# A hybrid attention block on one core: split probabilities in the last two blocks, row maxima moved by DMA, fused band operations, and a new order

## The chip, the core and the metric

The kernel runs on one core of a Trainium2 chip. The core has five engines with instruction streams of their own: TensorE (PE in the rows, PEld for its weight loads), VectorE (DVE), ScalarE (ACT), GpSimd (POOL) and SyncE (SP), which here only issues DMAs. They meet at semaphores. The metric is the device time of one execution in microseconds; lower is better.

## What is computed

One layer of a streaming encoder, 2048 positions of width 1024, in float32. Cut to what matters here:

```python
proj = jnp.einsum('bld,dc->blc', x, w_in)
qa, ka, va, ga, qi, ki, wi, qb, kb, vb, gb = jnp.split(proj, offsets, axis=-1)
# group A: an indexer scores keys, the top 256 are kept, attention over them with ALiBi
dots = jnp.einsum('bqhd,bsd->bqhs', qi_blk, ki)
score = jnp.einsum('bqh,bqhs->bqs', w_blk * idx_scale, jax.nn.relu(dots))
_, idx = lax.top_k(score, k_top)
logits = jnp.einsum('bqhd,bqkd->bqhk', q_blk, k_sel) * attn_scale - slopes * dist
p = jax.nn.softmax(logits, axis=-1)
ya = jnp.einsum('bqhk,bqkd->bqhd', p, v_sel)
# group B: a window of 2 chunks with a sink for each head
yb = sink_window_attention(qb, kb, vb, sinks, slopes[1::2])
y = jnp.concatenate([ya * jax.nn.silu(ga), yb * jax.nn.silu(gb)], axis=-1)
x = layer_norm(ALPHA * x + jnp.einsum('blc,cd->bld', y, w_out), ln_g, ln_b)
```

## The kernel before

The 2048 queries are 16 blocks (b) of 128. The work is written as pieces with names, and a planner in the kernel's file puts them in one order: each piece has an engine, an assumed duration, the pieces it needs and a preference from a table. Each engine then issues its pieces in that order, in program order, and waits on semaphores where it must. The names below are the planner's.

The first stage computes the projections (`product`, `norm`). Each product is made of three products of rounded parts (type fp32r, a value rounded to fewer bits): high x high, low x high and high x low; the parts are made on ACT (round), POOL and DVE (split). Beside it the indexer runs for pairs of blocks (p from 1 to 7): `dots` on PE, `relu` on ACT, `sum` on DVE, and then the search of the level of the 256th largest score: 32 steps a pair, `search` on DVE for one block of the pair and `sign` on ACT for the other (L1485, L1030). `masks` p ends a pair (L1503 to L1519); the masks go to DRAM and come back for their block.

Then, for each block b:

- the scan: `scan` on PE forms the logits of each head over up to 512 keys, `scan_max` on DVE adds the mask and takes the maximum in one fused instruction (L1582). `negate` (L1593 to L1596) joins the chunks' maxima and negates them, `minus_max` transposes them on PE (L1295), and `row_max` (L1603) multiplies the 8 rows by a 0/1 pattern `sel`, so that 8 rows of the operand `qa_ext` hold them, one for each head. The logits product then subtracts the maximum by itself.
- the units: for each key tile kt and half g of the heads, `logits` on PE (L1331 to L1333, at the diagonal also L1335 and L1336), `exp_a` on ACT (L1140) and `values` on PE (L1344), one product of plain float32, which the records show as two. Logits have two PSUM banks, probabilities three buffers: 272 units in all, 30 in block 14 and 32 in block 15.
- the tail: `leave_a`, `turn_a`, `y_a`, `columns_a`, `gate_a`, `store_a`.
- the band (group B): `window` on PE, `bias_b` on DVE twice a block, each an addition of the bias to 128x768 (L1562) and a maximum over it (L1564), `max_b` (L1569), `exp_b`, `turn_b`, `copy_b`, `mix_b`, `y_b`, `columns_b`, `gate_b`, `store_b`.

Behind the last values product stands the output product (L1390) with the layer norm.

## Time and profile before

| | |
|---|---|
| time, median of 3 runs | 1541.97 us (1541.08 to 1542.38) |
| the profiled execution | 1540.4 us, span 1538.6 us |
| PE busy | 1419.8 us (92%) |
| DVE busy | 1192.4 us (78%) |
| ACT busy | 932.3 us (61%) |
| POOL busy | 419.0 us (27%) |
| mean granted clock of PE | 0.967 of full speed |

The profile is of one execution. A busy share is an average over the whole span; what an engine waits for, and in which stage, is in the views of the trace. The granted clock is the share of full speed at which PE may run; below 1 the same product takes longer.

### The profile page before, as it was taken

The page shows a single profiled execution, that of the slowest core. Times are in us where ns is not written, and L with a number is a line of the kernel's source. Part 1 is how long each engine was busy: PE and PEld are TensorE (multiplying, and loading weights), DVE is VectorE, ACT ScalarE, POOL GpSimd, SP SyncE. Part 2 cuts the span into 40 slices and gives each one's busy share as a digit, 9 for nine tenths or more (in the row PEclk, how much of TensorE's full clock was granted, in tenths as well). Part 3 has the DMA queues.
Part 4 walks back from the last instruction along what each step waited for, and adds up shares of the span by engine and source line. Part 5 has one row for each costly group of instructions (what it writes and reads, how often), then busy time and mean ns, then how long its engine had stood idle before and what let it go on. Part 6 is the DMA issues. An engine that isn't in the chain of part 4 may idle for free.

```text
span 1538.6 us, 19197 instructions
## 1 busy us (share of the span) xinstructions
PE 1419.8 (92%) x6469; PEld 1031.3 (67%) x6520; DVE 1192.4 (78%) x2235; ACT 932.3 (61%) x1797; POOL 419.0 (27%) x268
## 2 busy tenths in 40 slices
PE   6998999799999976788999989999999999989997
PEld 5887888588787765455656656556565664468886
DVE  3477878879988967989999998999998770047776
ACT  3484966865964978457969746887995634301010
POOL 3332313643234324314122121121212601012221
PEclk9999999999999996798999999999999999999999
DMA  7331231531325245312132230222314412034442
GB/s 241 97 109 62 82 93 55 164 124 44 107 84 137 86 113 120 102 34 55 47 82 55 61 94 11 60 59 61 75 32 128 129 38 66 0 116 145 142 151 81
DMA packets 104306, 136.34 MB, mean 89 GB/s; under 512 B 6499, under 2 KB 81127, under 8 KB 103951
## 3 DMA queue, kind: packets, MB, share of 16 engines
q1 hardware_dynamic: 91344, 93.16, 22.0%
q10 hardware_dynamic: 9216, 31.20, 5.3%
q0 software_dynamic: 3648, 10.76, 2.3%
q8 instruction: 52, 0.85, 0.2%
q14 instruction: 46, 0.37, 0.1%
HBM read 92.76 MB, written 42.34 MB: 88 GB/s over the span
## 4 chain that ended last, share of the span: by engine, by line
PE 61%; DVE 17%; issue 8%; ACT 6%; POOL 4%; DMA 3%; ACTq 0%; SPq 0%; POOLq 0%; DVEq 0%
PE psum L1201 18%; PE psum L1390 9%; PE psum L1344 9%; PE psum L1272 4%; DVE above L1485 3%; PE psum L1332 3%; ACT above L1030 3%; PE psum L1333 3%; DVE score L1513 2%; PE psum L1217 2%; PE psum L1331 2%; PE psum L1232 2%; POOL w_lo L853 2%; PE psum L1234 2%; DMA x_raw<-xT 1%
## 5 line engine op out<-in xcount | busy, mean ns | idle before, releaser
L1485 DVE TENSOR_SCALAR_CACHE_REDUCE above<-dist,trial 128x512 bf16<-128x512 int32 (+13 forms) x224 | 345.9, 1544 | 6.1
L1030 ACT ACTIVATE above<-dist,trial 128x384 bf16<-128x384 int32 (+13 forms) x224 | 280.9, 1254 | 43.7 <-DVE trial L1458 27.1
L1201 PE MATMUL psum<-x_hi,w_hi 128*128 128x512 f32 x640 | 253.8, 397 | 32.4 <-DVE x_lo L1527 11.7
L1344 PE MATMUL psum<-prob,vw 128*65 128x512 f32 x544 | 270.2, 598 | 0.0
L1140 ACT ACTIVATE prob<-psum 128x512 f32<-128x512 f32 x272 | 158.4, 592 | 160.3 <-PE psum L1344 143.8
L1201 PE MATMUL psum<-x_lo,w_hi 128*128 128x512 f32 x640 | 251.2, 393 | 0.0
L1201 PE MATMUL psum<-x_hi,w_lo 128*128 128x512 f32 x640 | 251.1, 392 | 0.0
L1582 DVE CUSTOM_DVE_ANT_0 junk<-psum,mask 128x512 bf16<-128x512 f32 (+3 forms) x320 | 184.0, 606 | 21.7 <-PE psum L1275 11.4
L1201 PEld LDWEIGHTS psum<-x_hi,w_hi 128*128 128x128 f32 x640 | 121.3, 190 | 64.6 <-POOL w_lo L853 16.3
L1332 PE MATMUL psum<-qa_mix,ka_mix 128*128 128x512 f32 x272 | 162.0, 595 | 1.0 <-DVE qa_ext L1603 1.0
L1272 PE MATMUL psum<-ka_ext,qa_ext 128*128 128x512 f32 (+3 forms) x320 | 137.2, 470 | 19.1 <-DVE part_max L1582 10.4
L1201 PEld LDWEIGHTS psum<-x_hi,w_lo 128*128 128x128 f32 x640 | 121.3, 189 | 26.1
L1201 PEld LDWEIGHTS psum<-x_lo,w_hi 128*128 128x128 f32 x640 | 121.5, 190 | 24.0
L1064 ACT ACTIVATE relu<-psum 128x1024 f32<-128x1024 f32 (+1 forms) x76 | 71.1, 956 | 97.8 <-PE psum L1234 59.4
L845 POOL CAST w_hi<-raw 128x1024 fp32r<-128x1024 f32 x40 | 52.5, 1312 | 262.2 <-PE psum L1201 252.2
L1344 PEld LDWEIGHTS psum<-prob,vw 128*65 128x65 f32 x544 | 72.0, 138 | 62.9 <-issue 39.8
L1333 PE MATMUL psum<-qa_ext,ka_ext 128*128 128x512 f32 x272 | 109.3, 402 | 0.0
L853 POOL TENSOR_TENSOR w_lo<-raw,w_hi 128x1024 fp32r<-128x1024 f32 x40 | 106.0, 2649 | 5.8
L980 ACT ACTIVATE yt_hi<-yt_raw 128x1024 fp32r<-128x1024 f32 x16 | 16.9, 1059 | 148.4 <-PE psum L1390 117.5
L1390 PE MATMUL psum<-wo_hi,yt_hi 128*128 128x512 f32 x256 | 101.1, 395 | 5.2 <-POOL yt_lo L951 5.1
L1434 DVE SCALAR_TENSOR_TENSOR score<-relu,vw,score 128x512 f32<-128x512 f32 (+1 forms) x114 | 91.5, 803 | 12.0 <-ACT relu L1064 5.2
L1390 PE MATMUL psum<-wo_lo,yt_hi 128*128 128x512 f32 x256 | 100.7, 393 | 0.0
(154 smaller groups left out, 2818.0 us busy)
## 6 DMA issues: line engine op xcount, KB each, us to landing
raw<-w_tiles SPq DMA_DIRECT2D x40, 512.0 KB, 4.3
proj<-staged ACTq DMA_DIRECT2D x40, 512.0 KB, 3.6
qb_raw<-proj SPq DMA_DIRECT2D x32, 256.0 KB, 3.9
qa_raw<-proj SPq DMA_DIRECT2D x32, 256.0 KB, 4.4
yt_raw<-y_t SPq DMA_DIRECT2D x16, 512.0 KB, 5.2
x_row<-x_res SPq DMA_DIRECT2D x16, 512.0 KB, 3.9
out<-z ACTq DMA_DIRECT2D x16, 512.0 KB, 2.6
x_raw<-xT SPq DMA_DIRECT2D x12, 512.0 KB, 5.0
```

Source lines behind the costliest of these rows:

```text
L853: nc.gpsimd.tensor_tensor(w_lo[:, u, :, :].rearrange("p k c -> p (k c)"), raw[:, u, :], w_hi[:, u, :, :].bitcast(F32).rearrange("p k c -> ...
L1030: nc.scalar.activation(above[:, 0, 0:n], src, ACT.Sign, scale=-1.0, bias=u, accum_out=count[:, 0:1]).then_inc(sign_counted, 1)
L1140: nc.scalar.activation(prob[:, unit % 3, :], psum[:, 4 + unit % 2, :], ACT.Exp, scale=0.125).then_inc(a_prob, 1)
L1201: last = pe.matmul(psum[:, 2 * u + m, :], wt[:, u, k, :], xt[:, k, 512 * m:512 * m + 512], start=(k == 0 and q == 0), stop=(k == KT - 1 an ...
L1272: last = pe.matmul(psum[:, bank, 0:w], qa_ext[:, s, h, :], ka_ext[:, s, c:c + w], start=True, stop=not diag)
L1332: pe.matmul(o, ka_mix[:, ks], flat(qa_mix[:, s, hs, :]), start=False, stop=False)
L1333: last = pe.matmul(o, ka_ext[:, s, ks], flat(qa_ext[:, s, hs, :]), start=False, stop=(kt < b))
L1344: pe.matmul(psum[0:65, 6 + g, :], vw[:, kt, 0:65], prob[:, u % 3, :], start=(kt == 0), stop=(kt == b)).then_inc(a_used, 1)
L1390: last = pe.matmul(psum[:, 4 + 2 * s + m, :], yt[:, s, k, :], wt[:, k, cols], start=(k == 0 and q == 0), stop=(k == KT - 1 and q == 2))
L1434: v.scalar_tensor_tensor(o, relu[:, h, 0:w], wt, o, ALU.mult, ALU.add).then_inc(summed, 1)
L1485: v.tensor_scalar(above[:, 1, 0:n], src, u, None, ALU.is_ge, ALU.add, accum_out=count[:, 1:2]).then_inc(own_counted, 1)
L1582: v.tensor_tensor_reduce(out=junk[:, scan % 2, 0:w], in0=psum[:, scan % 2, 0:w], in1=mask[:, s, c:c + w], scale=1.0, scalar=-3.0e38, op0=A ...
```

## The change

Five things are changed together.

1. In blocks 14 and 15 (`SPLIT_FROM = 14`) the values product is made of three products of rounded parts. ACT computes the exponential twice, once in float32 and once rounded (`prob_hi`); the difference `prob_lo` is made on POOL for g = 0 and on DVE for g = 1 (`low_a`). The parts of the values are made once on POOL (`split_values`).
2. Row maxima: the multiplication by `sel` is gone. The maxima are transposed as they are (`turn_max`), DVE negates 8x128 of them into `minus_max` (`leave_max`), and SP moves these by DMA into one row of `qa_ext` (`place_max`). The negations ahead of the transposition are gone; up to block 3 the scan's maxima go straight to the transposed tile, from block 4 on one reduction (`top_of_chunks`) stays. The load and the copies of `sel` are gone.
3. `bias_b` adds and takes the maximum in one fused instruction for each head (four a half), and `y_a` has one reciprocal and one multiplication in place of two each.
4. `setup_dve` no longer waits for the last stores of the projections; the first `scan_max` does.
5. The DMA scratch is 2048 bytes a partition in place of the default. The assumed durations and the table of preferences are new, and a second table (`MOVE`) moves pieces against a first order. All pieces are put in a new order by this.

```diff
+SPLIT_FROM = 14
...
+                split = b >= split_from
+                add("ACT", 1.2 if split else 0.6, "exp_a", *unit, needs=[("logits", *unit), ("values", *unit_list[-3][1:])])
+                if split:
+                    add(*(("POOL", 1.33) if g == 0 else ("DVE", 0.66)), "low_a", *unit,
+                        needs=[("exp_a", *unit), ("low_a", *unit_list[-2][1:])])
+                add("PE", 0.66 if split else 0.86, "values", *unit,
+                    needs=[("exp_a", *unit), ("low_a", *unit), ("split_values", 1), ("leave_a", b - 1),
+                           ("values", *unit_list[-1][1:])])
...
+def first_ranks(plan):
+
+    base = whole_plan(NB)
+    first = base.timed(base.urgency())
+    like = {"low_a": lambda *unit: ("exp_a", *unit), "split_values": lambda i: ("split_qa", 8)}
+    return {piece: -first[like[piece[0]](*piece[1:]) if piece[0] in like else piece] for piece in plan.pieces}
+
...
+            def place_max(b):
+
+                sp.wait_ge(a_left_max, b + 1)
+                sp.dma_start(qa_ext[HD:HD + 1, b % 2, :, :].rearrange("p h q -> p (h q)").bitcast(F32),
+                             minus_max[:, :].bitcast(F32)) \
+                    .then_inc(a_ext, 16)
+
...
+            def split_values(i):
+                if i == 0:
+                    pool.wait_ge(norm_out, NB)
+                    settled()
+                    nc.gpsimd.tensor_copy(values_hi[:, :, :], vw[:, :, 0:65]).then_inc(values_hi_ok, 1)
+                    latest[0] = (values_hi_ok, 1)
+                else:
+                    settled()
+                    nc.gpsimd.tensor_tensor(values_lo[:, :, :], vw[:, :, 0:HD], values_hi[:, :, 0:HD].bitcast(F32),
+                                            ALU.subtract).then_inc(values_lo_ok, 1)
+                    latest[0] = (values_lo_ok, 1)
+
+            def low_a(b, kt, g):
+                u = units_to(b - 1) + 2 * kt + g
+                pool.wait_ge(a_prob, u + 1)
+                settled()
+                nc.gpsimd.tensor_tensor(prob_lo[:, u % 3, :], prob[:, u % 3, :],
+                                        prob_hi[:, u % 3, :].bitcast(F32), ALU.subtract).then_inc(a_low[0], 1)
+                latest[0] = (a_low[0], split_unit(b, kt) + 1)
+
...
-                nc.scalar.activation(prob[:, unit % 3, :], psum[:, 4 + unit % 2, :], ACT.Exp,
-                                     scale=0.125).then_inc(a_prob, 1)
+                last = nc.scalar.activation(prob[:, unit % 3, :], psum[:, 4 + unit % 2, :], ACT.Exp,
+                                            scale=0.125)
+                if b >= SPLIT_FROM:
+                    last = nc.scalar.activation(prob_hi[:, unit % 3, :], psum[:, 4 + unit % 2, :], ACT.Exp, scale=0.125)
+                last.then_inc(a_prob, 1)
...
-            def minus_max(b):
-
-                pe.wait_ge(a_neg, b + 1)
-                pe.transpose(psum[:, 0, 0:P], neg_max[:, :], ident[:, :]).then_inc(a_negt, 1)
+            def turn_max(b):
+
+                pe.wait_ge(a_scanned, scans_to(b))
+                if b >= 4:
+                    pe.wait_ge(a_top, b - 3)
+                if b == 0:
+                    pe.wait_ge(setup_pool, 2)
+                pe.transpose(psum[:, 0, 0:P], row_top[:, :], ident[:, :]).then_inc(a_turned_max, 1)
 
...
-                pe.matmul(psum[0:65, 6 + g, :], vw[:, kt, 0:65], prob[:, u % 3, :],
-                          start=(kt == 0), stop=(kt == b)).then_inc(a_used, 1)
+                if b < SPLIT_FROM:
+                    pe.matmul(psum[0:65, 6 + g, :], vw[:, kt, 0:65], prob[:, u % 3, :],
+                              start=(kt == 0), stop=(kt == b)).then_inc(a_used, 1)
+                    return
+                if (b, kt, g) == (SPLIT_FROM, 0, 0):
+                    pe.wait_ge(values_hi_ok, 1)
+                    pe.wait_ge(values_lo_ok, 1)
+                pe.matmul(psum[0:65, 6 + g, :], values_hi[:, kt, :], prob_hi[:, u % 3, :], start=(kt == 0), stop=False)
+                pe.matmul(psum[0:HD, 6 + g, :], values_lo[:, kt, :], prob_hi[:, u % 3, :], start=False, stop=False)
+                pe.wait_ge(a_low[g], split_unit(b, kt) + 1)
+                pe.matmul(psum[0:65, 6 + g, :], values_hi[:, kt, :], prob_lo[:, u % 3, :],
+                          start=False, stop=(kt == b)).then_inc(a_used, 1)
 
...
             def bias_b(b, g):
                 j0 = HD if b == 0 else 0
-                hs = slice(4 * g, 4 * g + 4)
                 dve.wait_ge(b_logits, 2 * b + g + 1)
                 if b:
                     dve.wait_ge(b_turned, 2 * b)
-                ps = psum[:, 2:4, 0:2 * WIN].rearrange("p b (h j) -> p b h j", h=2)[:, :, :, j0:WIN]
-                two = lambda t, j: t[:, hs, :].rearrange("p (b h) j -> p b h j", h=2)[:, :, :, j + j0:j + WIN]
                 if (b, g) == (0, 0):
                     dve.wait_ge(bias_in, 16)
                 if g == 0:
                     dve.wait_ge(sink_put, b + 1)
-                v.tensor_tensor(two(lb, HD), ps, two(bias, 0), ALU.add).then_inc(b_biased, 1)
-                dve.wait_ge(b_biased, 2 * b + g + 1)
-                small(v.tensor_reduce(mb[:, hs], lb[:, hs, HD + j0:HD + WIN + 1], AX_X, ALU.max))
+                for i in range(4):
+                    h = 4 * g + i
+                    last = v.tensor_tensor_reduce(out=lb[:, h, HD + j0:HD + WIN],
+                                                  in0=psum[:, 2 + i // 2, WIN * (i % 2) + j0:WIN * (i % 2) + WIN],
+                                                  in1=bias[:, h, j0:WIN], scale=1.0, scalar=sink8[:, h:h + 1],
+                                                  op0=ALU.add, op1=ALU.max, accum_out=mb[:, h:h + 1])
+                last.then_inc(b_biased, 1)
 
             def max_b(b):
                 if b:
                     dve.wait_ge(b_exp, 2 * b)
+                dve.wait_ge(b_biased, 2 * b + 2)
                 v.tensor_scalar(nmb[:, :], mb[:, :], -0.125, None, ALU.mult).then_inc(b_max, 1)
...
+                if scan == 0:
+                    for i in range(2):
+                        dve.wait_ge(stored[i], 16 * N_TILES)
...
+                top = part_max[:, h, c // 512:c // 512 + 1] if b >= 4 else row_top[:, h:h + 1]
                 v.tensor_tensor_reduce(out=junk[:, scan % 2, 0:w], in0=psum[:, scan % 2, 0:w],
                                        in1=mask[:, s, c:c + w],
                                        scale=1.0, scalar=-3.0e38, op0=ALU.add, op1=ALU.max,
-                                       accum_out=part_max[:, h, c // 512:c // 512 + 1]).then_inc(a_scanned, 1)
-
-            def negate(b):
+                                       accum_out=top).then_inc(a_scanned, 1)
+
+            def top_of_chunks(b):
                 dve.wait_ge(a_scanned, scans_to(b))
-                if b == 0:
-                    dve.wait_ge(setup_pool, 2)
-                n_chunks = 1 + b // 4
-                if n_chunks > 1:
-                    small(v.tensor_reduce(neg_max[:, 0:H], part_max[:, :, 0:n_chunks], AX_X, ALU.max))
-                    v.tensor_scalar(neg_max[:, 0:H], neg_max[:, 0:H], -1.0, None, ALU.mult).then_inc(a_neg, 1)
-                else:
-                    v.tensor_scalar(neg_max[:, 0:H], part_max[:, :, 0], -1.0, None, ALU.mult).then_inc(a_neg, 1)
-
-            def row_max(b):
-                s = b % 2
-                dve.wait_ge(a_negt, b + 1)
-                if b == 0:
-                    dve.wait_ge(setup_act, 1)
-                v.tensor_tensor(qa_ext[HD:HD + H, s, :, :], psum[0:H, 0, 0:P].unsqueeze(1).broadcast_to([H, H, P]),
-                                sel[:, :, :], ALU.mult).then_inc(a_ext, 1)
+                v.tensor_reduce(row_top[:, 0:H], part_max[:, :, 0:1 + b // 4], AX_X, ALU.max).then_inc(a_top, 1)
+
+            def leave_max(b):
+                dve.wait_ge(a_turned_max, b + 1)
+                if b:
+                    dve.wait_ge(a_ext, 16 * b)
+                v.tensor_scalar(minus_max[:, :], psum[0:H, 0, 0:P], -1.0, None, ALU.mult).then_inc(a_left_max, 1)
 
             def den_b_of(b):
                 dve.wait_ge(b_exp, 2 * b + 2)
...
+            def low_a(b, kt, g):
+                u = units_to(b - 1) + 2 * kt + g
+                dve.wait_ge(a_prob, u + 1)
+                v.tensor_tensor(prob_lo[:, u % 3, :], prob[:, u % 3, :], prob_hi[:, u % 3, :].bitcast(F32),
+                                ALU.subtract).then_inc(a_low[1], 1)
...
-    nc = bacc.Bacc("TRN2", target_bir_lowering=False, num_devices=1)
+    nc = bacc.Bacc("TRN2", target_bir_lowering=False, num_devices=1, dynamic_dma_scratch_size=2048)
```

PE's order in the middle of block 15. Before, the mask's product (L1331), the two logits products and then one values product, of the unit four ahead of these logits:

```order
L1344 MATMUL psum<-prob,vw 65x512
L1331 MATMUL psum<-ident,mask 128x512
L1332 MATMUL psum<-qa_mix,ka_mix 128x512
L1333 MATMUL psum<-qa_ext,ka_ext 128x512
L1344 MATMUL psum<-prob,vw 65x512
```

and now:

```order
L1424 MATMUL psum<-prob_hi,values_hi 65x512
L1425 MATMUL psum<-prob_hi,values_lo 64x512
L1427 MATMUL psum<-prob_lo,values_hi 65x512
L1404 MATMUL psum<-ident,mask 128x512
L1405 MATMUL psum<-qa_mix,ka_mix 128x512
L1406 MATMUL psum<-qa_ext,ka_ext 128x512
L1424 MATMUL psum<-prob_hi,values_hi 65x512
L1425 MATMUL psum<-prob_hi,values_lo 64x512
L1427 MATMUL psum<-prob_lo,values_hi 65x512
```

Three products stand where one stood; the turn of logits and values is the same.

DVE's order at the end of the scan of block 12, inside the search of the last pair (the row with `above,count` and the two behind it are one search step; "ISA" rows are the fused instruction and the read of its result). Before:

```order
L1582 ISA junk,part_max<-psum,mask 128x128
L1582 ISA part_max 128x1
L1593 TENSOR_REDUCE neg_max<-part_max 128x8
L1594 TENSOR_SCALAR neg_max<-neg_max 128x8
L1562 TENSOR_TENSOR lb<-psum,bias 128x4x192
L1564 TENSOR_REDUCE mb<-lb 128x4
L1569 TENSOR_SCALAR nmb<-mb 128x8
L1603 TENSOR_TENSOR qa_ext<-psum,sel 8x1024
```

and now:

```order
L1669 ISA part_max 128x1
L1676 TENSOR_REDUCE row_top<-part_max 128x8
L1568 TENSOR_SCALAR above,count<-dist,trial 128x2048
L1572 TENSOR_SCALAR accept<-count 128x1
L1575 TENSOR_SCALAR trial<-accept,trial 128x1
L1682 TENSOR_SCALAR minus_max<-psum 8x128
L1568 TENSOR_SCALAR above,count<-dist,trial 128x2048
L1572 TENSOR_SCALAR accept<-count 128x1
L1575 TENSOR_SCALAR trial<-accept,trial 128x1
```

The large multiplication became a small negation, and what stands between the reduction and it is a search step in place of half a band block.

SP's queue about the maxima of blocks 8 and 9, now. The new entry is `qa_ext<-minus_max`; whatever stands behind it is issued after it:

```order
L816 DMA qa_ext<-minus_max 1x8x128
L810 DMA mask<-masks 128x1280
L773 DMA qb_raw<-proj 64x8x128
L775 DMA kb_raw<-proj 64x2x192
```

Here the mask of block 9 and the queries of a band block stand behind the maxima of block 8.

## Rows read from the trace of the kernel before

**Rows 1.** The page: busy time by engine, and the chain that ended last.

```profile
PE 1419.8 (92%) x6469; PEld 1031.3 (67%) x6520; DVE 1192.4 (78%) x2235; ACT 932.3 (61%) x1797; POOL 419.0 (27%) x268
...
PE 61%; DVE 17%; issue 8%; ACT 6%; POOL 4%; DMA 3%; ACTq 0%; SPq 0%; POOLq 0%; DVEq 0%
```

**Rows 2.** Busy time by stretch; columns as in the first line.

```profile
core 0: us, PE busy (x) PEld busy (x) DVE busy (x) ACT busy (x) POOL busy (x), PEclk, DMA share, GB/s
...
580.00:1178.00 598.00, 544.97 (x2511) 350.72 (x2551) 553.71 (x1110) 446.52 (x847) 132.72 (x96) 0.95 0.25 62
1178.00:1262.00 84.00, 82.06 (x424) 55.59 (x429) 62.54 (x159) 45.52 (x98) 32.58 (x19) 1.00 0.36 109
1262.00:1354.00 92.00, 91.89 (x316) 48.10 (x320) 5.08 (x13) 33.55 (x54) 6.26 (x4) 1.00 0.10 32
```

**Rows 3.** Waits of DVE, 571 to 1178 us: in total, times, longest.

```profile
DVE junk L1582 <- PE psum L1275: 8.5, 14, 1.5
DVE mask L1542 <- DMA proj<-staged: 7.8, 1, 7.8
```

**Rows 4.** Busy time by stretch, the beginning of the middle stage.

```profile
580.00:600.00 20.00, 10.41 (x42) 9.35 (x43) 17.92 (x48) 17.82 (x43) 11.41 (x7) 0.50 0.62 131
600.00:720.00 120.00, 100.61 (x438) 65.66 (x443) 104.28 (x202) 74.41 (x124) 30.45 (x20) 0.90 0.24 61
```

**Rows 5.** Groups of DVE instructions by shape: busy us, mean ns, idle before.

```profile
L1564 DVE TENSOR_REDUCE mb<-lb 128x4 f32<-128x772 f32 x30 | 28.7, 957 | 1.0
L1562 DVE TENSOR_TENSOR lb<-psum,bias 128x768 f32<-128x768 f32 x30 | 28.6, 954 | 10.0 <-PE psum L1248 9.7
...
L1603 DVE TENSOR_TENSOR qa_ext<-psum,sel 8x1024 fp32r<-8x1024 f32 x16 | 19.5, 1216 | 1.6 <-PE psum L1295 1.1
...
L1582 DVE CUSTOM_DVE_ANT_0 junk<-psum,mask 128x256 bf16<-128x256 f32 x32 | 13.2, 419 | 5.1 <-PE psum L1275 5.1
...
L1594 DVE TENSOR_SCALAR neg_max<-neg_max 128x8 f32<-128x8 f32 x12 | 3.2, 266 | 0.4
...
L1596 DVE TENSOR_SCALAR neg_max<-part_max 128x8 f32<-128x8 f32 x4 | 2.1, 522 | 0.1
```

**Rows 6.** The timeline of DVE at 584.8 us: start, duration.

```profile
584.77 0.28 DVE L1582 CUSTOM_DVE_ANT_0 junk<-psum,mask 128x128 bf16<-128x128 f32 x1
...
584.98 0.28 DVE L1582 CUSTOM_DVE_ANT_0 junk<-psum,mask 128x128 bf16<-128x128 f32 x1
```

**Rows 7.** DMA issues: size, median us from issue to landing.

```profile
sink<-sinks SPq DMA_DIRECT2D x1, 4.0 KB, 3.1
...
ka_ext<-c_pos POOLq DMA_DIRECT2D x1, 2.0 KB, 3.6
```

**Rows 8.** The timeline of PE and ACT inside block 15.

```profile
1303.69 1.02 PE L1344 MATMUL psum<-prob,vw 128*65 128x512 f32 x2
...
1304.81 0.60 ACT L1140 ACTIVATE prob<-psum 128x512 f32<-128x512 f32 x1 [0.94 <-PE psum L1344]
...
1305.22 1.02 PE L1344 MATMUL psum<-prob,vw 128*65 128x512 f32 x2
1305.65 0.10 PEld L1331 LDWEIGHTS psum<-ident,mask 128*128 128x128 bf16 x1 [0.29 <-ACT prob L1140]
1306.08 0.38 PE L1331 MATMUL psum<-ident,mask 128*128 128x512 bf16 x1
...
1306.34 0.60 ACT L1140 ACTIVATE prob<-psum 128x512 f32<-128x512 f32 x1 [0.93 <-PE psum L1344]
```

**Rows 9.** The chain in order of time, one stretch of rounded products.

```profile
384.31 19.12 PE psum L1201 x84
```

**Rows 10.** The timeline of ACT at 1293 us: two exponentials in a row.

```profile
1293.36 1.06 ACT L1140 ACTIVATE prob<-psum 128x512 f32<-128x512 f32 x2
```

**Rows 11.** Groups of subtractions by shape, on POOL and on DVE.

```profile
L862 POOL TENSOR_TENSOR x_lo<-x_raw,x_hi 128x1024 fp32r<-128x1024 f32 x8 | 19.1, 2384 | 11.0 <-ACT x_hi L980 10.6
...
L1527 DVE TENSOR_TENSOR x_lo<-staged,x_hi 128x1024 fp32r<-128x1024 f32 x4 | 4.9, 1221 | 2.1 <-ACT x_hi L980 2.1
```

**Rows 12.** One line of DVE: duration ns shortest/median/longest.

```profile
L1569 DVE TENSOR_SCALAR nmb<-mb x16: 157/302/1894, 592.1 to 1245.8; 128x8 f32<-128x8 f32 x16
```

157 lines of the change are left out of this document (84 added, 73 removed).

## The prediction

> **What bounds the kernel now.** I read the page's busy shares and its chain first. PE is busy 92% of the span, DVE 78%, and the chain that ended last is PE for 61% and DVE for 17% [rows 1]. That is an average over stages, so the next view is the busy time of each engine by stage [rows 2]. The reader is to see five stages. Up to 560 us stand the input products, which the change touches only in their order. From 580 to 1178 stand searches, scans, bands and the units of blocks 0 to 12: PE is busy 545.0 of 598 us, DVE 553.7 of 598. From 1178, when the last mask is there, to 1262 PE is busy 82.1 of 84, and to 1354, where only the units of block 15 and the last of block 14 are left, 91.9 of 92. The rest is the output product, unchanged.
>
> In the middle stage, which of two nearly full engines sets the pace? The waits of DVE from 571 to 1178 us say it: the largest are 8.5 us on scans and 7.8 us once on the last stores (just ahead of 580) [rows 3]. Of the 44 us in which DVE has nothing running in the stage, most are the small steps between its own dependent instructions. PE is idle for 53 us there, and it also runs below full clock: 0.50 granted from 580 to 600 us, 0.90 from 600 to 720 [rows 4]. At a lower clock PE needs more time for the same work, so its true need is smaller than 545 us. So DVE sets the time at which the last mask is made, and PE the 176 us behind it.
>
> **The change part by part.** The sum is made against the profiled execution, 1540.4 us with a span of 1538.6; the median of the runs shown, 1542.0, lies 1.6 us higher, and I add that at the end.
>
> *Band operations on DVE.* Before, each half of a band block costs an addition of 0.954 us and a maximum of 0.957 us [rows 5]. Ahead of the last mask stand 26 halves: 26 x 1.91 = 49.7 us. Now each half is four fused ones of 128x192. The same kind of instruction takes 0.419 us at 128x256 [rows 5] and 0.28 us at 128x128, where the next starts 0.21 us behind it [rows 6]. Halfway in width that is 0.35 us, and 0.07 less from start to start: 0.28 at best, and 0.36 at worst, if a little of waiting comes to it. I take 0.32. The new order puts 28 halves ahead of the last mask: 28 x 4 x 0.32 = 35.8 us. Difference -13.9 (-18 to -9).
>
> *Row maxima.* The multiplication of 8x1024 that spreads the maxima costs 1.216 us a block [rows 5]; 14 stand ahead of the last mask, 17.0 us. In its place DVE negates 8x128 out of PSUM, which no row shows; the nearest small ones are 0.266 and 0.522 us [rows 5], and nothing at all would be below any row. I take 0.27: 3.8 us, difference -13.2 (-17.0 to -9.7). The old negations go: 10 x 0.266 + 4 x 0.522 = -4.7. The two DVE pairs of the tail that become one, and the reduction that stays, I count at nothing.
>
> So DVE has 31.8 us less ahead of the last mask (24 to 40). What does the stage get of it? PE's idle time there would fall from 53 to 21 us if all came through, and then PE's own waits count more often. I take four fifths, -25.
>
> *The last stores.* DVE no longer waits for them before its constants, 7.8 us [rows 3], but the first maximum of a scan still does, and the scans behind it wait for the same loads. In the new order five search steps stand between. Between 0 and -7.8 I take -2.
>
> *The path of the maxima.* From the transposition to the first unit of the block there stood one DVE instruction of 1.216 us. Now there are the negation (0.27), the issue on SP, and a transfer from 8 partitions to one. Of the small transfers one of 2 KB takes 3.6 us from issue to landing and the 4 KB of the sinks 3.1 [rows 7]; this one has 4 KB, so I take 3.1 and 3.6 as the upper end; under 1.2 it would be no loss, which no row comes near. The path is 0.27 + 3.1 - 1.2 = 2.2 us longer a block. The Trainium skill (DMA: Bandwidth & Descriptors, the table of where a transfer's time goes) gives a fixed cost of about 2.0 us to any transfer; by it the path would be some 1.1 us longer. PE has work between the transposition and the first unit in all blocks but 0, 1, 2, 4, 6, 10 and 12, where it is short (two or three scans, turns or index products). There PE waits up to 2.2 us more, 15 us at most, while DVE goes on with searches. That is in the fifth I took off. Behind the new SP entry its own queue stands still as well: loads of queries, gates and masks are issued later. They are mostly asked for a block ahead, so I take nothing.
>
> *The units of blocks 14 and 15.* A unit now starts 1.53 us after the one before (1303.69 to 1305.22), of which the values product has 0.86 (1305.22 to 1306.08) [rows 8]. Rounded products cost 19.12 / 84 = 0.228 us each [rows 9], three of them 0.68. Bound by PE, a unit would take 1.35, 0.18 less; 62 units make 11 us. But ACT now computes the exponential twice, and a pair in a row takes 1.06 us [rows 10]. PE's order is values u, logits u+4; these logits need the exponential of u+2, and that one the buffer which values u-1 frees. The loop over two units is: 0.26 from the end of that values product to ACT's start (1306.08 to 1306.34), 1.06 for ACT, 0.24 from ACT's end to the next weight load (1305.41 to 1305.65), 0.10 for that load, and a unit of 1.35: 3.01, or 1.51 a unit. The 0.24 may hold a wait of PE's own, so 1.51 is an upper value and 1.35 the lower; I take 1.49, near the loop and 0.04 less than before, for the 47 units that stand alone: -2. The 15 of block 14 that the new order puts beside scans get the full 0.18: -3. The low parts (POOL about 1.2 us, half of the 2.384 of 128x1024; DVE half of 1.221 [rows 11]) have more than a unit of time before their product, so they cost only behind the last one: +1. Together -4; the ends are -11 (PE bound) and +3 (an ACT pair of 1.2 us).
>
> A small DVE instruction of 8 columns takes between 0.157 and 1.894 us in this trace [rows 12]: something holds it. The Trainium skill (SBUF — State Buffer, on the shared port pair) says that VectorE with two SBUF inputs and a GpSimd instruction that reads SBUF exclude each other for a whole instruction, which the new subtractions on both engines would. Were each of the 31 on DVE held for a product of 1.2 us, that is 37 us of DVE time in stages where it is busy 62.5 of 84 and 5.1 of 92 us [rows 2], so nearly all of it would stay hidden. The smaller DMA scratch and the first 560 us I count at nothing, with +-3 for the new order.
>
> Sum: -25 - 2 - 4 = -31, so 1509.4 by the profiled execution and 1511 by the median.
>
> **The rivals.** *PE becomes the bound in the middle stage.* For it speaks that PE is at 91% there and gets new waits; against it its low clock, which leaves it time. If half of DVE's saving is lost (16 us) and the units give 2: about 1524, and up to 1539.
>
> *All passes, and PE's clock comes back.* The stage loses DVE's 37 us or more, and the stretches with a clock of 0.50 and 0.90 shrink (they cost half of 10.4 and a tenth of 100.6 us [rows 4], 15 us of PE time). With 8 us at the stores and 6 at the units: about 1490.
>
> *Slower: the maxima's transfer.* If no work covers it, 14 blocks x 2.2 = 31 us, as much as DVE saves; with PE's order standing still behind it and SP's loads late, each block of the middle stage costs 3 us or more. It decides once the exposed wait is over 2.2 us a block in every block. That gives about 1550. Against it speaks the work that stands between in half of the blocks.
>
> *Nothing.* The saving is eaten by these waits exactly: 1542.
>
> **How the numbers follow.** My forecast (1497 to 1524) gets 0.58, PE as the bound (1524 to 1539) 0.14, the better case (under 1497) 0.11, nothing 0.06, slower 0.11. The likeliest is 1511. The range from 1494 to 1541 leaves out most of the better case (0.08) and the slower one (0.11). Faster by over 0.2%, which is about what a measurement of this kernel can tell: 0.58 + 0.14 + 0.11 = 0.83; within it 0.06; slower 0.11.
>
> **What would show it.** The last mask at 1150 us instead of 1178 (right if at 1145 to 1160); fused band instructions of 0.30 to 0.36 us; units of block 15 at 1.46 to 1.52 us; 170 us from the last mask to 1354's counterpart instead of 176. Wrong would be: waits of PE for the new transfer of more than 15 us in sum; units above 1.55 us; a last mask later than 1170 us.

## The result and the profile after

The changed kernel takes 1529.28 us (median of 4 runs, 1527.82 to 1531.2) against 1542.18 (4 runs beside it): a ratio of 0.992, 95% interval 0.9906 to 0.9934. That is 12.9 us less, where 31 were forecast. The profiled execution of the changed kernel has a span of 1526.0 us, 12.6 less than before.

The page of the changed kernel, busy time by engine and the chain that ended last, answers to [rows 1]:

```profile
span 1526.0 us, 19664 instructions
...
PE 1411.9 (93%) x6530; PEld 1039.8 (68%) x6582; DVE 1183.7 (78%) x2410; ACT 959.2 (63%) x1857; POOL 458.1 (30%) x301
...
PE 60%; DVE 15%; ACT 12%; issue 6%; DMA 3%; POOL 2%; SPq 1%; ACTq 0%; DVEq 0%; POOLq 0%
```

DVE's busy time fell by only 8.7 us, but 24.0 us of new low parts are in it, so the edits took 32.7 us away over the whole kernel. The prediction counted 31.8 ahead of the last mask alone. There, from the start to the end of the last mask, DVE is busy 974.0 us instead of 997.9, 23.9 less; with the same code in before's order it is 968.2. So the new order puts more of DVE's other work ahead of the mask. PE's busy time fell by 7.9 us. The groups of DVE by shape (count, busy us, mean ns, idle before) answer to [rows 5]:

```profile
L1642 DVE CUSTOM_DVE_ANT_0 lb<-psum,bias,sink 128x192 f32<-128x192 f32 x120 | 42.9, 414 | 6.2 <-PE psum L1317 5.8
L1710 DVE TENSOR_TENSOR prob_lo<-prob,prob_hi 128x512 fp32r<-128x512 f32 x31 | 24.0, 774 | 45.6 <-ACT prob_hi L1209 45.5
```

The fused band instructions start every 0.34 us (604.90, 605.24, 605.58 in the timeline), near the 0.32 that was forecast.

Busy time by stretch, with the stages cut at the changed kernel's own marks, answers to [rows 2]:

```profile
core 0: us, PE busy (x) PEld busy (x) DVE busy (x) ACT busy (x) POOL busy (x), PEclk, DMA share, GB/s
580.00:1173.00 593.00, 545.20 (x2508) 350.45 (x2547) 526.61 (x1230) 458.25 (x878) 142.40 (x97) 0.96 0.24 62
1173.00:1262.00 89.00, 85.79 (x441) 58.80 (x449) 60.06 (x183) 51.55 (x99) 45.55 (x28) 0.98 0.41 128
1262.00:1345.00 83.00, 81.72 (x369) 51.03 (x374) 22.22 (x38) 51.67 (x94) 31.15 (x25) 1.00 0.04 13
```

The first line is the failure in one row. In the middle stage DVE is busy 526.6 us instead of 553.7, PE 545.2 instead of 545.0, and the stage is 593 us long instead of 598. DVE's 27 us became 22 us of idle time and 5 us of gain. The last mask is ready at 1173.1 us, the end of the second entry below, where the prediction had 1150. The same instruction ended at 1179.7 us before, so it came 6.6 us earlier, where 28 were forecast:

```profile
1163.55 5.03 DVE L1599 SCALAR_TENSOR_TENSOR dist<-score,dist 128x4096 f32<-128x4096 int16 x1
1168.62 4.47 DVE L1602 TENSOR_SCALAR above<-dist,trial 128x2048 bf16<-128x2048 f32 x2
```

What DVE waits for now, from 571 to 1173 us (total, times, longest), beside [rows 3]:

```profile
DVE junk L1669 <- PE psum L1341: 12.2, 17, 2.3
DVE junk L1669 <- PE psum L1344: 9.4, 10, 2.5
DVE junk L1669 <- issue: 5.9, 1, 5.9
DVE lb L1642 <- PE psum L1317: 4.7, 4, 1.8
```

The wait for the last stores (7.8 us) is gone, and nothing took its place: the first maximum of the scans starts at 578.5 us right behind a search step. The single wait of 5.9 us is another one, at 629.4 us, ahead of the first maximum of block 3, whose product starts at 628.7. All waits of DVE for PE in this stage together are 36.2 us; before they were 23.3. The scans' products, PE's, are the largest part of them.

To see where the gain is, I took three marks from the timelines: the start of the first product of a unit with the keys (F), the end of the last mask (M), and the start of the last such product (Z). Of the 12.6 us between the two profiles, 5.4 lie ahead of F (599.7 and 594.3 us), 1.2 between F and M (580.0 and 578.8), 3.8 between M and Z (158.3 and 154.5) and 2.2 behind Z. The profiles of kernels that are alike up to F put it anywhere from 592 to 601 us, so the 5.4 is rough; on average it is 595.7 in six profiles with the changed kernel's first part and 599.6 in four with before's, 3.9 us. The stage from which 25 us were to come gave 1.2.

### The profile page after: what moved, and what is told of

Its sections match the earlier page's. It is cut to its first block, busy times and chain, and to the rows that moved or that the text cites. A ratio compares the mean times of both kernels' runs of the same rounds, so it can differ in the third digit from the quotient of the medians.

```text
span 1526.0 us, 19664 instructions
## 1 busy us (share of the span) xinstructions
PE 1411.9 (93%) x6530; PEld 1039.8 (68%) x6582; DVE 1183.7 (78%) x2410; ACT 959.2 (63%) x1857; POOL 458.1 (30%) x301
## 4 chain that ended last, share of the span: by engine, by line
PE 60%; DVE 15%; ACT 12%; issue 6%; DMA 3%; POOL 2%; SPq 1%; ACTq 0%; DVEq 0%; POOLq 0%
PE psum L1270 17%; PE psum L1473 9%; PE psum L1418 7%; ACT above L1097 5%; PE psum L1341 4%; DVE above L1568 4%; PE psum L1405 3%; PE psum L1406 3%; PE psum L1404 2%; PE psum L1301 2%; PE psum L1286 2%; PE psum L1303 2%; DVE score L1596 2%; ACT accept L1103 2%; DVE score L1517 2%
## 5 line engine op out<-in xcount | busy, mean ns | idle before, releaser
L1418 PE MATMUL psum<-prob,vw 128*65 128x512 f32 x420 | 207.2, 595 | 1.8 <-ACT out_a L1047 1.8
L891 POOL CAST w_hi<-raw 128x1024 fp32r<-128x1024 f32 x40 | 43.5, 1087 | 297.1 <-PE psum L1270 290.8
L1341 PEld LDWEIGHTS psum<-ka_ext,qa_ext 128*128 128x128 f32 x320 | 62.4, 201 | 74.4 <-DVE part_max L1669 41.8
L899 POOL TENSOR_TENSOR w_lo<-raw,w_hi 128x1024 fp32r<-128x1024 f32 x40 | 102.3, 2557 | 5.8
```

What stands on the lines that cost most here:

```text
L899: nc.gpsimd.tensor_tensor(w_lo[:, u, :, :].rearrange("p k c -> p (k c)"), raw[:, u, :], w_hi[:, u, :, :].bitcast(F32).rearrange("p k c -> ...
L1341: last = pe.matmul(psum[:, bank, 0:w], qa_ext[:, s, h, :], ka_ext[:, s, c:c + w], start=True, stop=not diag)
L1418: pe.matmul(psum[0:65, 6 + g, :], vw[:, kt, 0:65], prob[:, u % 3, :], start=(kt == 0), stop=(kt == b)).then_inc(a_used, 1)
```

## The experiments

Theories at the start: the prediction's (DVE's work sets the time of the middle stage), the order of the changed kernel (it ate the gain, or made it), and TensorE's own work. The ratios are against the kernel before, 1542 us; differences of two ratios are given in us of it, with +-3 to 5 us by the intervals. F to M is from the profiled execution. "Low", the time at the lower clock, is explained further down; it is the mean of the timed runs.

| kernel | ratio, 95% interval | F to M, us | low, us |
|---|---|---|---|
| before | 1 | 580.0 | 102 |
| changed | 0.992, 0.9906 to 0.9934 | 578.8 | 98 |
| after_oldorder | 0.9997, 0.9979 to 1.0015 | 578.1 | 110 |
| before_in_new_order | 1.0146, 1.0124 to 1.0168 | 596.4 | 112 |
| in_new_order_fused | 1.0136, 1.0119 to 1.0153 | 597.4 | 121 |
| after_nosplit | 0.997, 0.9956 to 0.9983 | 579.4 | 101 |
| after_oldband | 0.9975, 0.996 to 0.999 | 586.5 | 110 |
| before_split | 1.0018, 1.0006 to 1.003 | 582.9 | 107 |
| before_fused | 0.996, 0.9944 to 0.9976 | 576.1 | 102 |
| before_maxima | 1.003, 1.0006 to 1.0054 | 584.9 | 108 |
| before_more_dve | 1.0067, 1.0044 to 1.009 | 592.9 | 107 |
| before_less_dve | 0.9984, 0.997 to 0.9998 | 577.3 | 102 |
| before_less_both | 0.996, 0.9939 to 0.9982 | 579.1 | 107 |
| after_more_dve | 0.9995, 0.9983 to 1.0007 | 588.4 | 100 |
| after_more_pe | 0.9952, 0.9936 to 0.9968 | 587.6 | 98 |
| after_less_dve | 0.9927, 0.9899 to 0.9954 | 579.9 | 105 |
| after_less_pe | 0.9945, 0.9927 to 0.9963 | 581.8 | 120 |
| after_less_both | 0.9909, 0.9889 to 0.9928 | 576.8 | 114 |
| after_filled_waits | 0.9899, 0.9882 to 0.9915 | 574.5 | 88 |
| after_filled_waits2 | 0.9888, 0.9871 to 0.9905 | 575.1 | 82 |

**Code and order taken apart.** The pieces' order was written out as a list and given to the other code.

```diff
-    order = planned_order()
+    order = written_order()
```

> The whole change, but its pieces in the order of before, each low part of a probability placed directly behind its exponential. Theory 1 (the order ate the gain): 1508 to 1520, the saving of VectorE comes back. Theory 2 (TensorE's work fills the time): as the changed kernel, 1524 to 1534. The prediction's theory: about 1511 to 1515, since 25 us of VectorE's saving should pass in either order.

Measured 0.9997, nothing gained: neither the prediction's 1511 to 1515 nor the first theory's 1508 to 1520, and worse than the changed kernel by 12 us. The second theory's 1524 to 1534 missed too.

> The code of before (band in two instructions a half, row maxima by a product on VectorE, one product with the values) in the order of the changed kernel; the two set-up pieces stand a few searches later, since before's set-up waits for stores that the changed kernel's does not. The changed code in before's order gained nothing (0.9997 of before) and the changed kernel without the split is at 0.997. Theory 1 (the order is itself the gain: it fills TensorE's short waits, whatever the code): 1533 to 1538, all of the gain that is not the split. Theory 2 (the order gains only with the time that VectorE has been freed): 1543 or more, slower than before, since VectorE would have 32 us more work ahead of the last mask, in an order made for less.

Measured 1.0146, +22.5 us: theory 2. So the same order costs before's code 22 us and gives the changed code 12. One caution: with the list word for word, before's code would wait for itself for ever. It needs its two set-up pieces later and a semaphore more, and its first unit starts at 607 us; 16 of the 22 us lie between F and M.

**One part at a time, in before's order.** The band's edit as in the diff; the split of the last two blocks as in the diff, each low part directly behind its exponential; the maxima's edit as in the diff, and with it the shorter set-up, the joined pairs of `y_a` and the small scratch.

> The kernel before with one edit of the change alone, the fused band instructions, in before's order: 14 us less of VectorE spread over all 16 blocks. The prediction's theory: -11, 1531. A1 (one-sided): 0 to -4. Undoing this edit in the changed kernel cost 8.5 us.

Measured 0.996, -6.2 us for 15.7 us less busy DVE, between the two expectations.

> The code and order of before with one part of the change alone: the probabilities of the last two blocks and the values in two rounded parts, three products. VectorE gets some 24 us of low parts, TensorE loses its float32 products. The prediction's price for this part is -4 us (1538, between 1531 and 1545). Theory 2, TensorE's work fills the time: TensorE's busy time fell 7.9 us from before to the changed kernel and nothing else in the change takes work from it, so -8 us, 1533 to 1536, that is, nearly the whole gain of the change. Theory 1 (the order ate the gain): about -4 us.

Measured 1.0018, +2.8 us: all the theories expected a gain. The waits of PE behind the last mask (1184 to 1300 us) show why:

```profile
PE psum L4931 <- DVE part_max L5251: 5.2, 6, 2.0
PE psum L4990 <- ACT prob_hi L4799: 1.1, 3, 0.4
PE psum L5013 <- POOL prob_lo L4560: 0.7, 1, 0.7
```

Before, the first of these is 1.2 us. While the scans of block 15 run beside the units of block 14, DVE has the low parts as well, and PE's idle time from M to Z rises from 1.9 to 9.2 us; a unit of block 14 takes 2.22 us on average instead of 2.05, one of block 15 1.42 instead of 1.48. The changed kernel's order has a unit of block 14 at 1.90 us and 3.1 us of idle time there.

> The kernel before in its own order with the row maxima's edit alone (maxima stored as they come, one negation into a row, a transfer instead of the product with the selector; setup shortened, small scratch): 18 us less VectorE by the prediction's working, of which four fifths would be -14, 1528. By the difference of the runs so far (whole change in this order -0.5, fused band -6.2, split +2.8) it should be about +3, 1545: the transfer's landing, or the order's places for these pieces, would then cost more than VectorE's saving gives. Between -2 and 0 would be the one-sided rule again, with nothing lost to the transfer.

Measured 1.003, +4.6 us: as the differences said, and DVE's 18.8 us (1192.4 to 1173.6 busy) gave nothing. PE's waits from 560 to 1186 us name the transfer:

```profile
PE psum L5035 <- DMA qa_ext<-minus_max: 5.3, 5, 2.0
PE psum L5034 <- DMA qa_ext<-minus_max: 3.9, 2, 2.4
```

That is 9.2 us for the transfer. In the kernel before PE waits 6.0 us for the multiplication in this place, and in the changed kernel 1.6 us for the transfer and 1.0 for the negation. The waits of PE of these two, 560 to 1186 us and the whole run:

```profile
PE psum L1272 <- DVE qa_ext L1603: 2.6, 2, 2.3
PE psum L1331 <- DVE qa_ext L1603: 2.4, 2, 1.5
PE psum L1332 <- DVE qa_ext L1603: 1.0, 2, 0.7
```

```profile
PE psum L1405 <- DMA qa_ext<-minus_max: 1.6, 2, 1.1
PE psum L1341 <- DVE minus_max L1682: 1.0, 1, 1.0
```

**One part at a time, in the new order.**

```diff
-                if b < SPLIT_FROM:
-                    pe.matmul(psum[0:65, 6 + g, :], vw[:, kt, 0:65], prob[:, u % 3, :],
-                              start=(kt == 0), stop=(kt == b)).then_inc(a_used, 1)
-                    return
...
+                pe.matmul(psum[0:65, 6 + g, :], vw[:, kt, 0:65], prob[:, u % 3, :],
+                          start=(kt == 0), stop=(kt == b)).then_inc(a_used, 1)
```

> The changed kernel in its own order, but the last two blocks' values product as one float32 product again, so that the band, the row maxima and the smaller scratch are what is left of the change. Theory 2 (TensorE's work fills the time): most of the gain goes, 1536 to 1540, for 24 us less work of VectorE. The prediction's theory: the split was worth 4 us, so 1533, with a range from 1526 to 1540. If VectorE's low parts hold up the last blocks, this kernel is faster than the changed one: 1524 or less.

Measured 0.997: the split is worth 7.7 us here, as theory 2 said, near twice the prediction's 4. Of it 6.5 us lie between M and Z (161.0 against 154.5).

> The changed kernel with the band as before, two instructions a half instead of the fused ones: some 14 us more work of VectorE, TensorE's unchanged. The prediction's theory (VectorE sets the time up to the last mask): +11 us over the changed kernel, 1540. TensorE's own work fills the time: 0 to +3, 1529 to 1532. In between means that VectorE and TensorE take turns.

Measured 0.9975, +8.5 us for 14.1 us more busy DVE.

> The code of before in the changed kernel's order (1565) with the fused band added: 15.7 us less VectorE. In that order VectorE's added work costs 0.6 to 0.8 of itself, so -10 to -13 from 1565, 1552 to 1555; the row maxima's edit (17 us of VectorE) would be the rest of the way to 1537, -15 to -18. If the maxima's edit costs time by its transfer, as in before's order (+3 to +5 us there), it would give less, and the band more: 1545 to 1550.

Measured 1.0136: the band alone gave 1.5 us of the 10 to 13, a miss. From there to 0.997 the maxima's edit with the shorter set-up, `y_a` and the scratch gives 25.6 us for 19.1 us less busy DVE. In before's order the same bundle cost 4.6. Each part's worth depends on the order and on what else stands in the queues.

**More and less work for one engine.** Work was added or left out in blocks 6 to 9 alone.

```diff
+                if 6 <= b <= 9 and c == 0:
+                    v.tensor_tensor(pad[:, h % 2, :], flat(bias[:, 0:2, :]), flat(bias[:, 2:4, :]), ALU.add)
                 dve.wait_ge(a_scan, scan + 1)
```

> The changed kernel with 32 more VectorE additions of 128x384 in blocks 6 to 9, one ahead of each head's first row maximum, into a buffer that nobody reads: at 0.4 to 0.5 us each 13 to 16 us more of VectorE, as much as the fused band saves, and none of TensorE. The prediction's theory: +10 to +15, 1539 to 1544. TensorE's work fills the time: 0 to +3. Both in turns: +4 to +9.

> The kernel before, in its own order, with the same 32 additions of 128x384 on VectorE in blocks 6 to 9 (15.0 us of busy time, which cost the changed kernel 11.7 us). Theory A (VectorE sets the time in either order, and before's order only happens to be unfit for the changed durations): +10 to +15, 1552 to 1557. Theory B (in before's order another engine sets the time, which would explain why the changed code gains nothing there): 0 to +4.

Measured +11.6 us (0.9995 against 0.992) for 15.0 us more busy DVE, and +10.3 us for 16.1. Work added to DVE passes by 0.6 to 0.8, in both orders.

```diff
+                if 6 <= b <= 9:
+                    pe.matmul(o, mask[:, s, ks], flat(ident4[:, :, :]), start=True, stop=True)
                 pe.matmul(o, mask[:, s, ks], flat(ident4[:, :, :]), start=True, stop=False)
```

> The changed kernel with the mask product of each unit of blocks 6 to 9 done twice: 68 more products of 128x512, at 0.215 us each from start to start 14.6 us more of TensorE, all ahead of the last mask or close behind it. VectorE sets the time there (the prediction's theory): 0 to +4. TensorE's work fills the time: +12 to +15, 1541 to 1544. Both fill it in turns: +5 to +11.

Measured +4.9 us for 14.6 us of added products (68 at the 0.215 us of the expectation), at the lower edge of "in turns".

```diff
                 w = min(512, n_keys - c)
+                if 6 <= b <= 9 and c == 0:
+                    w = P
```

> The kernel before with the first row maximum of each head in blocks 6 to 9 taken over 128 columns instead of 512 (the rest of those 32 chunks isn't looked at): about 0.4 us less each, some 13 us less of VectorE, nothing added. Theory A1 (each order is fitted so tightly to its durations that more work costs and less work gives nothing, because the next wait, on TensorE or ScalarE, is right behind): 0 to -3, though more work costs 10 or more. Theory A2 (VectorE alone sets the time, both ways): -9 to -13, about 1530; then the changed code's lost gain in before's order must lie in what the change adds (the transfer, the 24 us of low parts).

> The same narrowing of 32 row maxima in the changed kernel, in its own order. A1 (one-sided: more costs, less gives nothing): 0 to -3, 1526 to 1529. A2 (both ways): -9 to -13, about 1518.

Measured -2.5 us for 11.7 us less busy DVE, and +1.1 us (no difference) for 11.2. Work taken from DVE here passes by nothing to a fifth: A1 in both. The intervals leave room for a third, and for two fifths in before's order, but not for four fifths. The time goes into the next wait at once. The waits of DVE in the kernel with narrowed maxima, 571 to 1173 us, beside 9.4 and 12.2 us in the changed kernel:

```profile
DVE junk L1671 <- PE psum L1344: 21.7, 23, 6.7
DVE junk L1671 <- PE psum L1341: 15.0, 22, 2.3
```

DVE lost 11.2 us of work and waits 15.1 us longer for the scans' products. The prediction's four fifths fit work that is added in these blocks and not work that is taken away there.

```diff
-                pe.matmul(o, mask[:, s, ks], flat(ident4[:, :, :]), start=True, stop=False)
-                pe.matmul(o, ka_mix[:, ks], flat(qa_mix[:, s, hs, :]), start=False, stop=False)
+                if not 6 <= b <= 9:
+                    pe.matmul(o, mask[:, s, ks], flat(ident4[:, :, :]), start=True, stop=False)
+                pe.matmul(o, ka_mix[:, ks], flat(qa_mix[:, s, hs, :]), start=(6 <= b <= 9), stop=False)
```

> The changed kernel without the mask product in the units of blocks 6 to 9 (their logits miss the mask): 68 products of 128x512 less, 14.6 us at 0.215 us each. TensorE's work alone holds the stage: -11 to -15, 1515 to 1518. The engines hold it together through the order: -2 to -6, 1523 to 1527. As 14.6 us more cost 4.9 to 6.7 us, the same size downwards would mean that TensorE's share is the same both ways.

> The changed kernel with both cuts, the mask products of blocks 6 to 9 (14.6 us of TensorE) and the 32 narrowed row maxima (11 us of VectorE, which alone gave nothing). The engines hold the stage together: -9 to -12, 1517 to 1520, more than the two cuts alone add up to. TensorE alone: as without the mask products only, within 2 us of that run.

> The same two cuts in the kernel before, where the VectorE cut alone gave 2.5 us. Together: -9 to -13, 1529 to 1533. TensorE alone: -12 to -15 too, so this run speaks only beside the one without the mask products. Something else than these two engines (ScalarE, transfers): 0 to -5.

Measured +3.9, -1.7 and -6.2 us. All three missed. Less work of TensorE alone did not make the kernel faster; the 3.9 us slower is at the edge of the noise, since the two intervals just overlap. Beside the cut of DVE's work the same cut gave 2.8 us in the changed kernel and 3.7 in before. So TensorE's work in these blocks doesn't hold the stage in the simple sense. Busy time by stretch of the kernel without the mask products shows what changed:

```profile
580.00:720.00 140.00, 116.48 (x520) 81.18 (x529) 101.38 (x275) 95.58 (x180) 40.24 (x31) 0.84 0.33 80
720.00:900.00 180.00, 164.64 (x753) 105.72 (x753) 168.48 (x417) 150.52 (x294) 45.37 (x33) 0.93 0.24 63
900.00:1140.00 240.00, 229.14 (x1031) 145.51 (x1044) 225.14 (x507) 186.94 (x344) 44.95 (x32) 0.96 0.21 56
```

and of the changed kernel:

```profile
580.00:720.00 140.00, 119.88 (x534) 81.54 (x542) 100.93 (x263) 95.09 (x181) 42.92 (x32) 0.87 0.31 75
720.00:900.00 180.00, 169.46 (x816) 110.41 (x828) 169.55 (x419) 154.97 (x311) 44.19 (x31) 0.96 0.24 64
900.00:1140.00 240.00, 226.39 (x1036) 141.46 (x1052) 224.84 (x516) 186.30 (x343) 40.53 (x30) 0.99 0.22 57
```

From 720 to 1140 us there are fewer records of products (1784 for 1852), nearly the same busy time (393.8 for 395.9 us), and a granted clock of 0.93 and 0.96 instead of 0.96 and 0.99. The fewer products run longer at the lower clock. The difference is drawn a little large here: the profile of the kernel without mask products has 129 us at the lower clock, the mean of its runs is 120.

**The clock.** Windows of 5 us around the longest wait of PE in the stage, in the changed kernel, and below them PE's timeline:

```profile
655.00:660.00 5.00, 2.08 (x6) 0.52 (x4) 4.93 (x5) 1.19 (x2) 0.00 (x0) 0.96 0.51 119
660.00:665.00 5.00, 2.52 (x7) 2.14 (x8) 4.10 (x13) 0.00 (x0) 0.00 (x0) 0.50 0.36 143
665.00:670.00 5.00, 5.00 (x27) 3.42 (x27) 3.28 (x11) 0.60 (x1) 0.00 (x0) 0.86 0.00 0
670.00:675.00 5.00, 5.00 (x24) 3.29 (x22) 3.87 (x14) 2.11 (x3) 0.79 (x1) 1.00 0.35 108
```

```profile
655.21 1.88 PE L1418 MATMUL psum<-prob,vw 128*65 128x512 f32 x4
662.48 0.90 PE L1341 MATMUL psum<-ka_ext,qa_ext 128*128 128x512 f32 x2 [5.40 <-DVE part_max L1669]
...
663.40 0.65 PE L1404 MATMUL psum<-ident,mask 128*128 128x512 bf16 x1
663.49 0.99 PE L1405 MATMUL psum<-qa_mix,ka_mix 128*128 128x512 f32 x1
```

PE stands for 5.4 us, because DVE is at the masks and behind them at the index sums. From 659.6 us on the granted clock is 0.50, the lower of the two levels (1.2 of 2.4 GHz), and it stays there until about 666.4 us, 4 us after PE has work again. A mask product shows 0.65 us and not 0.39. Between 560 and 1180 us the changed kernel has 65 us at the lower level, by such windows of 5 us with 2 x (1 - clock) of each; the kernel before has 75, the one without mask products 92, the one with narrowed maxima 82 (in a profile with 116 us over the whole span, where the mean of its runs is 105), with both cuts 85, with more DVE work 55. The column "low" in the table is the same over the whole span, from the mean clock of every timed run.

What is 1 us of it worth? The runs of one and the same kernel differ in it too. Taken kernel by kernel, over 219 timed runs of the 20 kernels (two far outliers left out), a run with 1 us more at the lower clock is 0.25 us longer (+-0.05). This is worked out from each run's time and mean clock, and shows company, not cause.

To tell cause from company, the waits were filled with products that nobody reads, written to 32 partitions that the values banks leave free:

```diff
+                for i in range({(1, 0, 0): 8, (4, 1, 0): 20, (6, 1, 0): 9, (10, 0, 1024): 20}.get((b, h, c), 0)):
+                    pe.matmul(psum[96:128, 7, :], ident4[:, 0, 0:32], flat(ident4[:, :, :]), start=True, stop=True)
                 if (h, c) == (0, 0):
                     pe.wait_ge(qa_round, b + 1)
```

(the first of the two kernels without the entry of block 1)

> The changed kernel with 49 products more of TensorE that nobody reads (into the 32 unused partitions of a values bank), 10.5 us of work, 20, 9 and 20 of them at the head of the third row-maxima product of blocks 4, 6 and 10, where TensorE waits 5.4, 2.5 and 5.3 us for VectorE, which is at the masks. If the clock is a cause: the low stretches behind these waits (some 7 us each, with TensorE busy and at half speed) go, worth up to 3.4 us each: -4 to -10, 1519 to 1525. If the clock only goes along, or the engine does not count: 0 to +3, since the products lie in waits.

> As the one before, with 8 more of these products at the head of block 1's first row-maxima product, a wait of 4.0 us at 589 us, in which the clock is already low (8 x 0.43 = 3.4 us). The clock a cause: 0 to -3 us against the one before. If it only goes along: the same as that one.

Measured 0.9899 and 0.9888: 3.2 and 4.9 us faster than the changed kernel, with 11.1 and 14.7 us more work on its busiest engine (49 products, and 57 of which the first 8 run at the lower clock). The interval of the second (to 0.9905) only just doesn't meet that of the changed kernel (from 0.9906); the first's overlaps it. The low time falls from 98 to 88 and 82 us. Half of the difference (5 and 8 us) is the most that PE can win, and 0.25 of it (2.7 and 4.3 us) is near what was measured. The same windows and PE's timeline in the second kernel:

```profile
655.00:660.00 5.00, 4.46 (x21) 1.83 (x20) 4.79 (x7) 0.60 (x1) 0.00 (x0) 1.00 0.50 172
660.00:665.00 5.00, 4.47 (x28) 3.45 (x29) 4.57 (x19) 0.28 (x1) 0.00 (x0) 1.00 0.01 3
```

```profile
654.98 4.49 PE L1330 MATMUL psum<-ident 128*32 128x512 bf16 x20
660.43 0.56 PE L1343 MATMUL psum<-ka_ext,qa_ext 128*128 128x512 f32 x2 [0.96 <-DVE part_max L1671]
...
660.95 0.39 PE L1406 MATMUL psum<-ident,mask 128*128 128x512 bf16 x1
660.98 0.58 PE L1407 MATMUL psum<-qa_mix,ka_mix 128*128 128x512 f32 x1
```

So the clock is a cause: with the waits filled, the low stretch behind them is gone and the kernel is faster, though it does more. This kernel beats both, with 1521.8 us as its median beside 1540.0 for the kernel before.

## Why the prediction was wrong

*"DVE sets the time at which the last mask is made", and of its saving "I take four fifths, -25".* This step failed. The stage between the first unit and the last mask became 1.2 us shorter, and the mask came at 1173.1 us, where the prediction itself called anything behind 1170 wrong. The smaller fault is the size: the new order leaves 23.9 us of the 31.8 ahead of the mask. The larger one is what passes. The argument compared two busy times, 553.7 and 545.0 us of 598, and took the engine with 9 us more as the bound. It called most of DVE's 44 idle us small steps between its own instructions. That was a misreading: of the 44, 31.6 are waits for others, 23.3 of them for PE, and 12.7 are small steps. DVE was waiting for PE already, and with less work it waited more, 36.2 us. Two engines so close, with their orders fixed and waits on each other all through the stage, pass on added work of DVE (0.6 to 0.8 of it) and little of removed work (0 to 0.2 in blocks 6 to 9, 0.4 for the band in before's order).

*The order.* The prediction gave the new order +-3 us. It costs before's code 22 us, and it is worth 12 to the changed code. So the result can be read as a sum: +22.5 for the order, -27.1 for the band, the maxima and the set-up in it (from 1.0146 to 0.997, for 32.1 us less busy DVE), and -7.7 for the split. In this order and for these edits four fifths do pass over the whole kernel (between F and M 17.0 us for 26.3); the forecast left out the first term. In before's order the parts are -6.2 for the band, +4.6 for the maxima's edit and +2.8 for the split, and the whole gains nothing. No part has a price of its own. In the profile of before's code in the new order the first unit is 7.5 us later. Whether the set-up pieces that had to move are the cause stays open, and so does how much of the 25.6 us is DVE's time of the maxima. A fitting reading is that each order is made for the durations of its own code, so that what is longer than planned costs and what is shorter gives little; no run here shows it apart.

*The clock.* The prediction said that at a lower clock PE's "true need is smaller than 545 us", and so set PE aside. In the change itself the clock hardly moved: the low time is 98 us for 102. In the cuts it worked against the saving. Without the mask products the low time is 21 us longer. At half of it, an upper bound since PE doesn't always set the pace, the clock took 10.7 us and the cut gave 6.8; at 0.25 the clock took 5.3 and the cut gave 1.4. For the narrowed maxima (7 us longer) the clock took 3.5 and the cut gave 2.4, or 1.7 and 0.6. So the clock takes part of the saving back, but even without it most of the removed work would not have passed. The filled waits show this cause directly; for the two cuts the shares are only worked out.

*The last stores, -2.* Rather more: the 7.8 us are gone, and the first maximum waits for nothing. The first unit starts 5.4 us earlier in the two profiles and 3.9 on the average of ten; how much of it is this edit and how much the order, no run shows.

*The path of the maxima.* Counted as 2.2 us longer a block, by a transfer of 3.1 us. In blocks 4 and 12, where nothing else is in the way, the first product of a unit starts 2.1 us behind the end of the negation, issue included, so the path is 0.27 + 2.1 - 1.2 = 1.2 us longer. By the Trainium skill (DMA: Bandwidth & Descriptors, the table in the anatomy of one DMA, which it gives for transfers issued by GpSimd), a fixed cost of about 2.0 us, it was 1.1. This transfer is issued by SP; the trace agrees with that figure and not with the row that I took. Waits of more than 15 us would have spoken against the forecast. From the start of the negation, or of the multiplication before, to the first unit PE is idle 11.6 us in all 16 blocks, and 10.0 before. So the rival, slower, is out for the changed kernel. In before's order the same edit makes it 20.2 us and the kernel 4.6 us slower: there it was right in kind.

*The units, -4.* The mechanism was right, the size was not: 7.7 us. The usual step from unit to unit in block 15 is 1.40 us, where 1.49 was forecast and 1.53 stood before (1.54 with one product in the same order). The loop over two units is closed by ACT as predicted, since PE's next weight load waits for its second exponential, but its links are shorter:

```profile
1299.93 0.59 ACT L1209 ACTIVATE prob_hi<-psum 128x512 fp32r<-128x512 f32 x1
1300.59 0.10 PEld L1404 LDWEIGHTS psum<-ident,mask 128*128 128x128 bf16 x1 [0.33 <-ACT prob_hi L1209]
1300.85 0.60 ACT L1206 ACTIVATE prob<-psum 128x512 f32<-128x512 f32 x1 [0.32 <-PE psum L1427]
```

From ACT's end to the weight load it is 0.07 us, not 0.24, and from the end of the values product (1300.75) to ACT 0.10, not 0.26. The low parts on DVE take 0.69 us alone. The hold by GpSimd that the prediction spoke of is there in 3 of 31, which take 0.91, 1.17 and 2.56 us; the longest of them:

```profile
1257.14 2.39 POOL L1017 TENSOR_TENSOR yt_lo<-yt_raw,yt_hi 128x1024 fp32r<-128x1024 f32 x1 [1.56 <-ACT yt_hi L1047]
1257.52 2.56 DVE L1710 TENSOR_TENSOR prob_lo<-prob,prob_hi 128x512 fp32r<-128x512 f32 x1
```

DVE's subtraction ends 0.55 us behind GpSimd's (1260.08 and 1259.53), so it seems to have stood still until then; in the other two it is 0.55 us as well. (With the split alone in before's order 9 of 31 take 0.88 us or more.) In all it is 2.6 us of DVE's time and not 37, since the two engines' turns seldom meet. From the last mask to the end of the last values product it takes 158.9 us, against 163.9 before: 5.0 less, where the prediction had 6 (170 for 176).

*The rivals.* "PE becomes the bound" named 1524 to 1539 and holds the result, 1529. Its half of the saving lost was far more than half, and the order is not in it. "All passes, and PE's clock comes back" failed on both: 1.2 us passed, and the low time fell by 4 us. That 1529 lies between 1494 and 1541 is luck in part: of the 12.6 us in the profiles only 1.2 come from the stage that was to give 25.

## What to carry to other kernels

Where two engines are both above 90% busy and wait for each other in a fixed order, ask for the price of less work and of more work apart: here, in the same four blocks, more cost 0.6 to 0.8 of itself and less gave 0 to 0.2, so undoing an edit says little of what making it gives. This is no rule for every order: in an order that cost before's code 22 us, less work gave 0.84 of itself, set-up included. A cheaper edit wants its own order before it is judged. Before an engine is called the bound, add up what it waits for. Look at the granted clock behind every long wait of TensorE: a wait may cost more than its length, and work that nobody needs can be worth its place there.

## Not expected of the hardware

- After a wait of 5.4 us TensorE's clock is at its lower level and stays there some 4 us into the next work, in which the record of a mask product shows 0.65 us and not 0.39; with 20 idle products in that wait (4.49 us) the granted clock stays at 1.00.
- 14.7 us of added products made the kernel 4.9 us faster, and 14.6 us of products left out did not make it faster (3.9 us slower, at the edge of the noise).
- A subtraction of 128x512 on VectorE takes 0.69 us, and 2.56 us when GpSimd has begun one of 128x1024 just before it.
- A transfer of 4 KB from 8 partitions into one row was ready for TensorE 2.1 us behind the instruction that made its data, while the list of transfers gave 3.1 us for one of the same size.
